# Earlier residual rows, paced weight sums and moved conversions in a fused decoder block on eight cores

## The reference, cut to what matters

```python
h = rms_norm(x, norm_mix_pre)
u_a, v_a, q, k, v_b, g_a, g_b = split(h @ w_in)
y_a = chunked_spatial_gating(gelu(u_a), gelu(v_a), w_s, b_s, ln_v_g, ln_v_b)
y_b = dilated_attention_mixture(q * q_scale, k, v_b)
merged = sigmoid(g_a + b0) * (y_a @ w_a_proj) + sigmoid(g_b + b1) * (y_b @ w_b_proj)
x = x + rms_norm(merged @ w_out, norm_mix_post)          # "x1", 2048 x 1024 rows
h = rms_norm(x, norm_ffn_pre)
f = square(relu(h @ w_ff1)) @ w_ff2                      # 1024 -> 4096 -> 1024
x = x + rms_norm(f, norm_ffn_post)                       # the last residual
```

## Time and profile before

| | us |
|---|---|
| median of 3 runs (range) | 1240.79 (1240.14 to 1242.63) |
| the profiled execution | 1239.19 |
| its span, slowest core (cores from 1227.1) | 1237.7 |
| TensorE busy | 1120.9 (91%) |
| VectorE busy | 740.3 (60%) |
| ScalarE busy | 529.3 (43%) |
| GpSimd busy | 139.8 (11%) |
| DMA, mean rate over the span | 160 GB/s |

### The profile page before, as it was taken

One profiled execution on the slowest core, in us unless ns is written; L12 is line 12 of the kernel. 1 busy time (PEld: TensorE's weight loads), 2 busy tenths in 40 slices (PEclk: granted clock), 3 DMA queues, 4 the chain that ended last, 5 costly groups with the idle time before them and its releaser, 6 DMA issues.

```text
span 1237.7 us, 20810 instructions; the slowest of 8 cores (1227.1 to 1237.7 us)
## 1 busy us (share of the span) xinstructions
PE 1120.9 (91%) x7304; PEld 565.4 (46%) x7304; DVE 740.3 (60%) x1229; ACT 529.3 (43%) x797; POOL 139.8 (11%) x267
## 2 busy tenths in 40 slices
PE   4799999999597899899989999999999969999990
PEld 2376555665354345444434444444444423444440
DVE  5757777777575654965442346987743357773252
ACT  5437887778565763121112145653310213431120
POOL 0000000012022230000000013510000230000032
PEclk9899999999899999999999999999999988999995
DMA  9467878878747557589962228474454475454424
GB/s 234 129 153 144 169 143 149 149 133 151 125 70 116 126 133 156 166 246 282 251 170 41 46 82 288 167 222 157 160 178 151 158 242 204 150 178 159 167 79 162
DMA packets 92391, 197.55 MB, mean 160 GB/s; under 512 B 39041, under 2 KB 55553, under 8 KB 87426
## 3 DMA queue, kind: packets, MB, share of 16 engines
q1 hardware_dynamic: 79682, 141.69, 36.9%
q0 software_dynamic: 12608, 54.53, 24.0%
HBM read 194.11 MB, written 56.62 MB: 203 GB/s over the span
## 4 chain that ended last, share of the span: by engine, by line
PE 70%; DMA 13%; DVE 6%; issue 4%; ACT 4%; POOL 2%; SPq 0%; DVEq 0%; POOLq 0%; ACTq 0%
PE pst L195 70%; DMA sb_PB<-w_bf 6%; ACT sb_Et L629 2%; DMA sb_xi<-x_scr 2%; DMA sb_BS<-b_s 1%; DMA out<-sb_xi 1%; DMA sb_wva<-w_va 1%; DMA sb_xt<-x 1%; DVE sb_PB L889 1%; PE pst L199 1%; DVE sb_xi L1172 1%; ACT sb_Lr L700 0%; DVE sb_xn L491 0%; ACT sb_junk L484 0%; POOL sb_st L1165 0%
## 5 line engine op out<-in xcount | busy, mean ns | idle before, releaser
L629 ACT ACTIVATE sb_Et<-pst 128x1024 bf16<-128x1024 f32 (+1 forms) x160 | 150.3, 973 | 44.2 <-PE pst L195 33.5
L195 PE MATMUL pst<-sb_r,sb_hid 128*128 128x512 bf16 x640 | 139.1, 379 | 0.0
L641 DVE TENSOR_TENSOR sb_PT<-sb_Et,sb_EB 128x1024 bf16<-128x1024 bf16 (+2 forms) x200 | 110.2, 569 | 38.3 <-ACT sb_Et L629 25.1
L195 PE MATMUL pst<-sb_hT,sb_wqk 128*128 128x512 bf16 x512 | 126.2, 393 | 0.9 <-DVE sb_hT L497 0.9
L195 PE MATMUL pst<-sb_merged,sb_r 128*128 128x512 bf16 x512 | 123.0, 383 | 3.5 <-DVE sb_hid L1067 2.8
L923 ACT ACTIVATE sb_sg<-pst,sb_small 128x512 f32<-128x512 f32 x64 | 44.0, 687 | 181.9 <-PE pst L195 124.6
L195 PE MATMUL pst<-sb_hT,sb_wg 128*128 128x512 bf16 x512 | 116.7, 379 | 0.0
L195 PE MATMUL pst<-sb_TB,sb_r 128*128 128x512 bf16 x384 | 96.9, 390 | 8.9 <-ACT sb_sn L1064 7.7
L1064 ACT ACTIVATE sb_sn<-pst 128x512 f32<-128x512 f32 x96 | 57.1, 597 | 111.1 <-PE pst L195 99.7
L195 PEld LDWEIGHTS pst<-sb_r,sb_hid 128*128 128x128 bf16 x640 | 62.6, 98 | 75.6
L195 PEld LDWEIGHTS pst<-sb_merged,sb_r 128*128 128x128 bf16 x512 | 50.1, 99 | 64.9 <-issue 7.6
(11 more groups left out here) (116 smaller groups left out, 1594.2 us busy)
## 6 DMA issues: line engine op xcount, KB each, us to landing
w_bf<-w POOLq DMA_DIRECT2D x32, 512.0 KB, 8.5
sb_PB<-w_bf SPq DMA_DIRECT2D x32, 512.0 KB, 7.2
w_comb<-sb_PB SPq DMA_DIRECT2D x32, 512.0 KB, 5.7
sb_r<-w_comb SPq DMA_DIRECT2D x32, 512.0 KB, 4.0
sb_r<-w_comb SPq DMA_DIRECT2D x16, 1024.0 KB, 5.0
sb_r<-w_bf SPq DMA_DIRECT2D x32, 384.0 KB, 3.4
sb_r<-w_bf SPq DMA_DIRECT2D x12, 1024.0 KB, 5.1
sb_xt<-x SPq DMA_DIRECT2D x16, 512.0 KB, 12.6
```

Of the source, the lines that this page charges most:

```text
L195: e.matmul(out, lhsT=l, rhs=r, start=st, stop=sp, skip_group_check=True))
L629: P.act(lambda e: e.activation(out=et[:, :, 0:W], in_=psall[:, sb:sb + 2, 0:W], func=AF.Exp, scale=0.125), 2 * W, [], [et.key()], [sb, sb ...
L641: P.dve(lambda e: e.tensor_tensor(out=o, in0=i0, in1=i1, op=ALU.mult), n, rk, [pt.key()], rate=2, name="mask")
```

## The change

**The last residual.** `fin` takes one of ten row buffers: eight lie in h2T's space (`hx`, four per token half, free once the first product of that half is through), two are the old ones. `xorder` says which tile takes which; in the first half two buffers are used twice. The load is issued on SP's queue with a priority of its own, the store remains on POOL's. The first two small POOL operations become one (line 1171), since `gfin` is multiplied by sqrt(DM) once, on VectorE (line 1026). The sn buffers of group g are `3 * g + j + 8` modulo 12.

**The preparations.** The load gets `after=anchor[0]`, and the anchor is now the iteration's operation at line 933 of the new file (the `mA` one) instead of a matmul group; so the load of preparation n can't be issued before iteration n has come that far. Its `lat` in the plan is 9.0.

**The conversions.** 24 remain in head pairs 0 to 5, four each. Eight are added in the u projection, one per g, each after the gelu of that g's last window.

```diff
-            if conv:
+            if hp < 6:
                 P.prio = b0 + (11 + 3 * c) * 5 + 1
                 conv.pop(0)()
...
         anchor[0] = P.ops[-1]
+        if conv:
+            P.prio = U0 + 10 * g + 4
+            conv.pop(0)()
...
-    def prep(n, prio):
+    def prep(n, prio, after):
...
-                  [P.nkey(("w1b", g))], [ki], prio=prio)
+                  [P.nkey(("w1b", g))], [ki], prio=prio, after=after, lat=9.0)
...
-                    anchor[0] = P.ops[-2]
+                    anchor[0] = P.ops[-1]
...
-            prep(it, G0 + 20 * cb + 5 * w - (6 if it else 0))
+            prep(it, G0 + 20 * cb + 5 * w - (6 if it else 0), anchor[0])
...
-    xi = [buf(f"xi{i}", (176 + 4 * i) * K, [1024], F32) for i in range(2)]
+    xb = [buf(f"xi{i}", (176 + 4 * i) * K, [2, 512], F32) for i in range(2)]
+    hx = buf("hx", 64 * K, [8, 2, 512], F32)
+    xis = [(f"xh{s}_{j}", (lambda a, s=s, j=j: hx[:, 2 * j + a, s, :]), hx[:, 2 * j:2 * j + 2, s, :], hx.key((2 * j, 2 * j + 2), s),
+            [hx.key(2 * j + a, s) for a in range(2)]) for s in range(2) for j in range(4)]
+    xis += [(f"xb{j}", (lambda a, j=j: xb[j][:, a, :]), xb[j][:], xb[j].key(), [xb[j].key(a) for a in range(2)]) for j in range(2)]
+    xorder = [[0, 1, 2, 3, 8, 9, 0, 1], [0, 1, 2, 3, 4, 5, 6, 7]]
...
+    P.dve(lambda e: e.tensor_scalar(out=gfin[:], in0=gfin[:], scalar1=math.sqrt(DM), scalar2=0.0, op0=ALU.mult, op1=ALU.add), 1024, [gfin.key()],
+          [gfin.key()], prio=L0 - 4, rate=2)
...
-            s1, u2, u3 = [sn[(3 * (g % 4) + j)] for j in range(3)]
+            s1, u2, u3 = [sn[(3 * g + j + 8) % 12] for j in range(3)]
...
-                    P.dma("pool", lambda e: e.dma_start(out=x_[:], in_=x1_d[i]), 512e3, f"xi{i % 2}", [P.nkey(("x1", i))], [kx], prio=P.prio - 12)
-                    P.pool(lambda e: e.tensor_tensor(out=sp_[:, c0 + 2:c0 + 3], in0=sp_[:, c0:c0 + 1], in1=sp_[:, c0 + 1:c0 + 2], op=ALU.add), 0.25,
-                           [sp_.key((c0, c0 + 2))], [sp_.key((c0 + 2, c0 + 3))])
-                    P.pool(lambda e: e.tensor_scalar(out=sp_[:, c0 + 2:c0 + 3], in0=sp_[:, c0 + 2:c0 + 3], scalar1=1.0 / DM, scalar2=EPS,
-                                                     op0=ALU.mult, op1=ALU.add), 0.25, [sp_.key((c0 + 2, c0 + 3))], [sp_.key((c0 + 2, c0 + 3))])
+                    xc, xh, xa, kx, kh = xis[xorder[s][(4 if c0 == 8 else 0) + p]]
+                    P.dma("sp", lambda e: e.dma_start(out=xa, in_=x1_d[i].rearrange("p (a c) -> p a c", a=2)), 512e3, xc + "l",
+                          [P.nkey(("x1", i))], [kx], prio=F2 + (10 if c0 == 12 else 30) + p)
+                    P.pool(lambda e: e.tensor_scalar(out=sp_[:, c0 + 2:c0 + 3], in0=sp_[:, c0:c0 + 1], scalar1=sp_[:, c0 + 1:c0 + 2], scalar2=DM * EPS,
+                                                     op0=ALU.add, op1=ALU.add), 0.25, [sp_.key((c0, c0 + 2))], [sp_.key((c0 + 2, c0 + 3))])
```

More of the change, by code:

```diff
@@ L215, in dma @@
         cost = (0.45 if q != "pool" else 0.7) * len(fns)
-        o = self._add(q, list(fns), cost, reads, writes, prio, nb=nbytes, chan=chan, lat=2.0, name=name)
+        o = self._add(q, list(fns), cost, reads, writes, prio, nb=nbytes, chan=chan, lat=lat, name=name)
         if after is not None:
```

12 lines of the change are left out of this document (5 added, 7 removed).

## The result

The changed kernel takes **1198.97 us** (median of four runs, 1197.87 to 1199.69) where the kernel before takes 1240.92 beside it: a ratio of 0.9659, 95% interval 0.9643 to 0.9676. The forecast was 1200.6, the range 1186 to 1216.

What follows compares the result with a forecast made beforehand. TensorE, busy in nearly every slice, was taken to bound the kernel, so only its waits and low-clock places counted. Gains less costs summed to 40.2 us: 1239.19 to 1199.0, plus 1.6 for the median, 1200.6 us; range 1186 to 1216.

Steps and rivals of the forecast that it cites:

- Tail: After the last matmul: ten row buffers bring residual rows before the sums; gain 12.6 us, bounds 9 and 14.7.
- Boundary: Between the token halves, where 18.2 us were lost: earlier residual rows and rotated sn buffers gain 14.2 us (9.7 to 18.2).
- The 4.0 us that were kept for VectorE's leftover work: At the halves' boundary: loss still expected from 8.5 us of VectorE work left when the next first product begins; 0 to 8.5.
- Gate and gating loops: Preparations behind the gating loop end TensorE's waits and low clock there; gain 10.5 us (5.2 to 11.5).
- the sign I had given: Gate and gating loops: no TensorE wait over 1 us between 500 and 700 after the change.
- BS and wva: Loads beside the last two head pairs: with eight conversions gone, BS gains 5.9 us (3 to 5.9), wva 1.0 (0 to 10.2).
- 1.0 for the u projection: Cost of eight conversions added on GpSimd's queue in the u projection, taken near zero from 0 to 8.5 us.
- a term of 0: wva load: by the ring-order rule, removing a conversion issued after it gains nothing; the forecast itself took 1.0 us.
- Output projection: Two preparations and the scaling of gfin added to VectorE's queue there; cost 3.0 us, bounds 0 to 4.6.
- The forecast case: Whole kernel: the summed terms hold, 1200.6 us; chance 0.46.
- VectorE takes over: Rival for the whole kernel: VectorE is late wherever it can be, 25.1 us of gain remain, 1215.7 us; chance 0.23.
- the mark of an error: Output projection: growth by more than 5 us would show the prediction wrong.

Runs made afterwards that it cites:

- rows_two: old_sn with all residual rows through two buffers instead of ten, loads still on SP's queue: 1214.6 us, ratio 0.9761.
- rows_poolq: The changed kernel with the residual rows' loads issued on GpSimd's queue instead of SP's, ten buffers kept: 1202.8 us, ratio 0.9686.
- old_stat: The changed kernel with the old three small statistics operations and without the scaling of gfin on VectorE: 1196.6 us, ratio 0.9632.
- no_rows: The changed kernel with two old residual buffers, loads on GpSimd's queue, old statistics and old sn rotation; pacing and conversions stay changed: 1221.4 us, ratio 0.9844.
- old_sn: The changed kernel with the old rotation of the sn buffers, 3 (g mod 4) + j, in both halves: 1189.2 us, ratio 0.9573.
- no_conv: The changed kernel with the conversions back in all eight head pairs and none in the u projection: 1205.5 us (two executions).
- rows_only: The changed kernel without the preparations' pacing and without the moved conversions, so the rows part alone with the new sn rotation: 1217.7 us, ratio 0.978.
- conv_five: old_sn with four more conversions moved: none in the sixth head pair, twelve in the u projection: 1187.4 us, ratio 0.9547.
- sn_half: The changed kernel with the old sn rotation in the first token half and the new one in the second: 1190.0 us, ratio 0.9581.

## Why the prediction was right, and where it was not

The profiled executions differ by 1237.7 - 1196.3 = 41.4 us, against a sum of 40.2. By its terms (profiled cores, behind them the medians of the cores):

- **Tail, 12.6 predicted, 13.8 measured (14.6).** VectorE's work came out as built up: from 1161.99 to 1187.9 it is 25.9 us, predicted 26.3. rows_two shows that the number of buffers was the main cause (11.7 us). The term that was off is what follows the last store's issue, taken over at 9.06 us and measured at 7.9: GpSimd's closing DRAIN became shorter when the loads left its queue. By rows_poolq that is 1.3 us, and old_stat adds 0.6 for the small operation that I had put at zero; 11.7 + 1.3 + 0.6 = 13.6 is nearly the 13.7 by which no_rows and the changed kernel differ in the tail.
- **Boundary, 14.2 predicted, 18.3 measured (16.8).** The 4.0 us that were kept for VectorE's leftover work did not occur. The first groups of the next half run ahead into free banks, with either rotation (old_sn 193.7), so the rotation, which I counted as part of this gain, gave nothing. The number of buffers gave 13.4 us (rows_two), and the move of the loads to SP's queue, which I had put at nothing, 3.1 (rows_poolq).
- **Gate and gating loops, 10.5 predicted, 9.8 measured (9.6).** Right in the gating loop. In the gate loop one wait of 1.80 us remained, against the sign I had given: I had read the waits of 1.62 and 1.94 us before as the price of sums between the evictions. But VectorE is busy without a break from 505.86 to 508.80 in the changed kernel, with the gate's own evictions and products (its rows from 507.19 on are shown above), and TensorE waits 1.80 us for the last of them. Before, one single sum of 0.42 us (516.25, shown above) stood in the wait of 1.94. The two waits together fell from 3.56 us to 2.58, where I had taken away all of it. The low clock behind them did go (1.89 us for 8 matmuls instead of 3.40). What I had not seen is that the pacing guards against the moved conversions: the two parts were priced apart, and only together they are what the sum says.
- **BS and wva, 6.9 less 1.0 for the u projection, 7.4 measured from the start to the first u product (3.4 as a median).** The wait for BS was 4.1 us on the profiled core of before and 0.9 to 4.1 over the cores, so that the term from one core was too large for a typical one; no_conv measured the whole at 6.5. BS itself landed 12.3 to 17.5 us after its issue over the cores before, and 4.2 to 6.1 in the changed kernel. The wait for wva fell from 6.3 to 5.1 as medians of the cores, 1.2 us for the predicted 1.0. The other kernels say that this is on the small side. The last load of wva landed 14.2, 15.2 and 15.7 us after its issue in the three kernels with the conversions in place (before, no_conv, rows_only; medians of the cores), and 10.8 to 13.4 in the ten with eight moved, 12.7 in the middle. So the conversion issued 5.8 us behind that load cost it some 2.5 us. The Trainium skill says ("DMA: Bandwidth & Descriptors", section "Queues, rings and completion order") that each DMA engine consumes one queue's descriptors in ring order, from which I had worked out a term of 0; the runs don't bear that out. What was issued ahead counts for more: in conv_five, where the four of the sixth head pair went too, the load landed after 7.4 us. In the u projection, where I had taken a conversion's landing of 8.5 us as the upper end of a cost, it was 17.7, and yet no cost is seen.
- **Output projection, -3.0 predicted, -7.9 measured (-6.2), outside its bounds of 0 to 4.6.** This is the step of the prediction that failed, in its cause too. I priced VectorE's added operations. With all of them in place old_sn and sn_half are at 281.1, as the kernel before is at 281.5, so no cost of theirs is left. What cost 6 us is the line on the sn buffers, which I read only for the boundary. I did not look up what lies under the buffers that group 0 now takes.

The sum came out within 1.2 us by luck: 4.1 us too little at the boundary, 1.2 in the tail and 1.5 before the u projection stood against 4.9 too little for the output projection's cost and 0.7 too much for the loops. The forecast case held; of the rivals "VectorE takes over" had no place where it was seen. Of the signs four did not come as named: the wait of 1.80 us in the gate loop; 193.9 us between the second products instead of about 198; ten waits, together 8.0 us, in the output projection instead of one or two of a microsecond; and its growth by more than the 5 us that I had named as the mark of an error.

The other rule, "Issuing engines are not separate DMA queues" of the same page of the Trainium skill, says that DMAs run on the same 16 DMA engines whoever issues them. I had made of it that the move of the loads from GpSimd to SP is worth nothing. For the transfers the trace agrees: the last store lands 3.2 us after its issue either way. But the issuing engine's list is not free. rows_poolq is 3.8 us slower, of which the boundary's 3.1 come from loads that stand in GpSimd's list ahead of the statistics, and the tail's 1.3 are its DRAIN.

## What to carry to other kernels

Before a buffer rotation is changed, look up what lay at its addresses: in a kernel that overlays buffers, the first user of a new phase inherits the waits of the old one. When work is postponed, look at what consumes its result, and in whose queue that consumer stands; a conversion in an idle-looking stage is free only if the in-order engine that needs it comes late enough. A DMA that waits in an engine's list holds up that engine's other work, so look at what else the issuing engine has to do. A gain of the right size can hide two errors of opposite sign, so compare stage by stage, over all cores, not the sum.
